# State-space mask: from TensorE's masking passes to a product on GpSimd and a minimum on VectorE

## What is computed

```python
def ssd_chunked_scan(xs, dt, a, bm, cm):
    ...
    a_cum = jnp.cumsum(jnp.moveaxis(adt, 2, -1), axis=-1)
    ...
    causal = jnp.tril(jnp.ones((CHUNK, CHUNK), dtype=bool))
    seg = a_cum[..., :, None] - a_cum[..., None, :]
    decay = jnp.where(causal, jnp.exp(jnp.where(causal, seg, 0.0)), 0.0)
    cb = jnp.einsum('bclgn,bcsgn->bcgls', cc, bc)
    y_diag = jnp.einsum('bcgrls,bcsgrp->bclgrp', cb[:, :, :, None] * decay, xdt)
    ...
    y_off = jnp.einsum('bclgn,bcgrpn,bcgrl->bclgrp', cc, h_prev, jnp.exp(a_cum))
    return (y_diag + y_off).reshape(b_, s_, h_, p_)
```

## Times and profile before

| | us |
|---|---|
| median of 3 runs | 1275.12 (1274.4 to 1275.44) |
| the profiled execution | 1276.14 |
| its span, from first to last instruction | 1274.4 |
| TensorE busy | 1253.2 (98%) |
| VectorE busy | 858.9 (67%) |
| ScalarE busy | 515.6 (40%) |
| GpSimd busy | 114.0 (9%) |
| transfers | 71.94 MB, 56 GB/s |

### The profile page before, as it was taken

The page is one execution under the profiler, slowest core; times in us unless marked ns, Lnnn a source line. Parts: engine busy times, 40 slices in busy tenths (PEclk is TensorE's granted clock), DMA queues, the critical chain, the costliest instruction groups (busy, mean ns, idle before and its releaser), DMA issues.

```text
span 1274.4 us, 16374 instructions
## 1 busy us (share of the span) xinstructions
PE 1253.2 (98%) x6120; PEld 1011.3 (79%) x6120; DVE 858.9 (67%) x1090; ACT 515.6 (40%) x794; POOL 114.0 (9%) x69
## 2 busy tenths in 40 slices
PE   7999999999999999999999999999999999999997
PEld 6777777777886888888778888888888888888886
DVE  4546656646397546634787878777787778787863
ACT  5435535547674225213433332424232423233441
POOL 0000000062300002600000000000000000000018
PEclk9999999999999999999999999999999999999999
DMA  6111101110004122110220211112111211010113
GB/s 245 50 34 34 33 33 34 33 50 17 1 1 151 64 70 83 63 34 7 77 67 33 67 37 63 49 49 66 34 65 52 77 35 66 33 66 33 66 58 125
DMA packets 22804, 71.94 MB, mean 56 GB/s; under 512 B 2528, under 2 KB 2784, under 8 KB 22752
## 3 DMA queue, kind: packets, MB, share of 16 engines
q1 hardware_dynamic: 22752, 71.22, 16.3%
HBM read 67.02 MB, written 4.19 MB: 56 GB/s over the span
## 4 chain that ended last, share of the span: by engine, by line
PE 46%; DVE 4%; issue 1%; ACT 1%; DMA 0%; DVEq 0%; SPq 0%; ACTq 0%
PE ps L1090 9%; PE ps L1091 9%; PE ps L1092 9%; PE ps L736 5%; PE ps L737 5%; PE ps L738 5%; PE ps L1130 1%; PE ps L1128 1%; PE ps L1129 1%; DVE w_lo L607 1%; DVE conv_ff L1994 1%; PE ps L1116 1%; DVE conv_ff L1990 1%; ACT conv_ff L1515 0%; DVE conv_ff L2001 0%
## 5 line engine op out<-in xcount | busy, mean ns | idle before, releaser
L736 PE MATMUL ps<-x_hi,w_hi 128*128 128x512 f32 x336 | 139.1, 414 | 7.9 <-DVE x_lo L1711 7.2
L1090 PE MATMUL ps<-mix_hi,w_hi 128*128 128x512 f32 x352 | 137.3, 390 | 1.9 <-DVE partial L2021 1.8
L1091 PE MATMUL ps<-mix_lo,w_hi 128*128 128x512 f32 x352 | 137.0, 389 | 0.0
L1092 PE MATMUL ps<-mix_hi,w_lo 128*128 128x512 f32 x352 | 137.0, 389 | 0.0
L738 PE MATMUL ps<-x_hi,w_lo 128*128 128x512 f32 x336 | 132.4, 394 | 0.0
L737 PE MATMUL ps<-x_lo,w_hi 128*128 128x512 f32 x336 | 131.8, 392 | 0.0
L736 PE MATMUL ps<-h_hi,w_hi 128*128 128x512 f32 x288 | 112.5, 391 | 0.7 <-DVE acc L2042 0.6
L737 PE MATMUL ps<-h_lo,w_hi 128*128 128x512 f32 x288 | 112.1, 389 | 0.0
L738 PE MATMUL ps<-h_hi,w_lo 128*128 128x512 f32 x288 | 112.1, 389 | 0.0
L2042 DVE TENSOR_TENSOR acc<-acc,ps 128x512 f32<-128x512 f32 x144 | 94.6, 682 | 24.9 <-PE ps L738 24.5
L602 ACT ACTIVATE w_hi<-weight_sums 128x512 fp32r<-128x512 f32 x44 | 27.8, 632 | 200.5 <-PE ps L738 149.9
(11 more groups left out here) (264 smaller groups left out, 2652.5 us busy)
## 6 DMA issues: line engine op xcount, KB each, us to landing
raw<-u_up SPq DMA_DIRECT2D x44, 512.0 KB, 3.3
raw<-u_in SPq DMA_DIRECT2D x22, 512.0 KB, 3.2
down_raw<-u_down SPq DMA_DIRECT2D x38, 256.0 KB, 2.8
x_stage<-u_x SPq DMA_DIRECT2D x8, 512.0 KB, 8.8
raw<-u_out SPq DMA_DIRECT2D x8, 512.0 KB, 3.2
x_nat<-x_nat SPq DMA_DIRECT2D x8, 512.0 KB, 3.3
raw<-u_gate SPq DMA_DIRECT2D x8, 512.0 KB, 3.2
out<-o_norm SPq DMA_DIRECT2D x7, 512.0 KB, 2.6
```

The lines of the kernel that those rows point to most:

```text
L736: mm(dst, w_hi, x_hi, start=first, stop=False)
L1090: mm(dst, w_h[:, k], t_h[:, kt, :], start=fresh and kt == 0, stop=False, skip_group_check=True)
L1091: mm(dst, w_h[:, k], t_l[:, kt, :], start=False, stop=False, skip_group_check=True)
L1092: last = mm(dst, w_l[:, k], t_h[:, kt, :], start=False, stop=kt == 3, skip_group_check=True)
```

## The change

TensorE's masking products go, with their tables `ident_r` and `mask_r`, the semaphore `cexp_done` and ScalarE's wait. Instead GpSimd multiplies the block `cb` of each group, in place, with the table of ones on and below the diagonal, once ScalarE has copied it out of PSUM; `masked` now counts these. The first of the two products stands ahead of `gate(9)`, the second behind it. The exponentials above the diagonal are no longer zero and may be large or infinite, so VectorE takes the minimum with one in the instruction that multiplies with `cb`. VectorE's `attended_low(1)` moves behind the states.

```diff
-MASK_BEFORE = {"cu1": 0, "st2": 1, "cb1": 2, "yy0": 3}
-MASK_INSIDE = {4: 4, 6: 5}
...
-        def mask(h):
-
-            eng.wait_ge(cexp_done, h + 1)
-            dst = two(task_place("cu%d" % h)[0])
-            for b in range(2):
-                last = mm(dst[:, b * HALF:(b + 1) * HALF].rearrange("p (k n) -> p k n", k=4), ident_r[:, :],
-                          mask_r[:, :].unsqueeze(1).broadcast_to([P, 4, P]), start=False, stop=True, skip_group_check=True)
-            last.then_inc(masked, 1)
...
-            if name in MASK_BEFORE:
-                mask(MASK_BEFORE[name])
...
-                              start=c % 4 == 0, stop=False, skip_group_check=True)
+                              start=c % 4 == 0, stop=c % 4 == 3, skip_group_check=True)
...
-                    if i == 0 and c in MASK_INSIDE:
-                        mask(MASK_INSIDE[c])
...
-            act(ce[h][:, :], src, ACT.Exp).then_inc(cexp_done, 1)
+            act(ce[h][:, :], src, ACT.Exp)
...
-            eng.wait_ge(masked, h + 1)
...
-        v.tensor_copy(ident_r[:, :], table("ident"))
-        v.tensor_scalar(mask_r[:, :], table("cap_le"), 0.0, 32768.0, ALU.min, ALU.mult)
...
-            evacuated("cb%d" % g)
-            v.tensor_tensor(wt[h][:, :], wt[h][:, :], cb[:, g, :], ALU.mult)
+            eng.wait_ge(masked, g + 1)
+            v.scalar_tensor_tensor(out=wt[h][:, :], in0=wt[h][:, :], scalar=1.0, in1=cb[:, g, :],
+                                   op0=ALU.min, op1=ALU.mult)
...
                 attended_low(0)
-                attended_low(1)
...
+        attended_low(1)
         attended_low(2)
...
+        def masked_products(k):
+            pair, before = task_place("cb%d" % k)
+            eng.wait_ge(d_free[pair], before + 1)
+            block = cb[:, k, :].rearrange("p (m n) -> p m n", m=MT)
+            g.tensor_tensor(block, block, table("tri_le").unsqueeze(1).broadcast_to([P, MT, P]),
+                            ALU.mult).then_inc(masked, 1)
+
+        masked_products(0)
         gate(9)
+        masked_products(1)
```

More of the change, by code:

```diff
@@ L321, in build @@
     un_b = put("weights_t1", [P, HALF], F32, top[0] - 4 * HALF)
-    mask_r = put("mask", [P, P], F32R)
     zero = put("zero", [P, 1])
@@ L325, in build @@
     cap_gt = put("cap_gt", [P, P])
-    ident_r = put("ident_r", [P, P], F32R)
     pool_w = put("pool_w", [P, 2, P])
@@ L451, in build @@
     decay_done = sem("decay_done")
-    cexp_done, masked, wt_done = sem("cexp_done"), sem("masked"), sem("wt_done")
+    masked, wt_done = sem("masked"), sem("wt_done")
     xdt_done = sem("xdt_done")
```

## The result

The changed kernel is slower. Its first four runs have a median of 1282.42 us (1280.6 to 1284.1) against 1274.8 us of the kernel before on the same chip: a ratio of 1.0054 [1.0042, 1.0067], or 1282.0 us on the scale of the median of 1275.12. Two later measurements of the same kernel gave 1280.96 us (1.0043 [1.0029, 1.0057]) and 1281.4 us (1.0046 [1.0032, 1.0059]). The profiled execution took 1280.6 us, the lowest of the four; its span is 1278.8 us.

A forecast was written before the change was run, and what follows sets the result against it. VectorE's queue was taken to bound the SSD stage; stalls from GpSimd's two products and gate 9, less gains at the first low half and states, summed to +4.1 us on the 1275.12 median: 1279.2 us, range 1277.2 to 1282.2.

The forecast's parts named there:

- The exclusion: SSD stage: a VectorE step with two SBUF inputs and a GpSimd product wait for each other; losses 1.45, 1.45, 2.2 us.

The follow-up runs named there:

- x5_again: The changed kernel measured again without an edit: 1280.96 us, ratio 1.0043.
- x3_lowback: The changed kernel with attention low half 1 back at its old place ahead of the states of pair 1: 1280.7 us, ratio 1.0045.
- x1_fill: The changed kernel with seven plain f32 matmuls filling TensorE's pause before the first value product: 1280.28 us, ratio 1.0042.
- x6_fill_both: The changed kernel with two f32 products ahead of the second group's block and three ahead of the first value product on TensorE: 1281.21 us, ratio 1.0044.

## What to carry to other kernels

An idle GpSimd is not free help while VectorE's steps with two SBUF inputs set the stage: a 1024-column product of 2.4 us on it costs VectorE 1.4 to 2.2 us, more than the 1.22 us of doing it on VectorE itself, and best of all is a place where VectorE waits. Before work is taken off an engine that is 98% busy, read what that engine waits for at the end of the stage: here it was VectorE, and 3.6 us of matmuls were worth 0.2 us of the stage. Before a step is moved, look at which wait it fills at its old place.

## What the runs showed of the hardware

- GpSimd's fills (0.95 us for 1024 columns) leave VectorE's two-input steps at 0.56 us; its products stretch them to 2.0 to 2.58. The exclusion is in reading.
- With both queues full GpSimd gets its turn behind the VectorE step that runs, and a step of 1.22 us then takes 3.37.
- GpSimd's product takes 2.35 us when it has the way free and longer when a step of VectorE runs at its start: 2.66 for gate 9 at 353.29, up to 3.29 for the second product (x5_again).
- The granted clock fell to half at pauses of TensorE of 2.0 to 3.4 us, within the pause or some 1 us behind it at most: at 3.40 us in the changed kernel, at 2.97 and 1.99 in x5_again, at 2.27 in x3_lowback. It did not fall at each of them: the pause of 2.97 us before 359.46 was followed by sixteen matmuls in 2.02 us, and the same pause in x1_fill by the same matmuls in 3.65. In the trace of x6_fill_both, with pauses of 0.9 us, it did not fall.
